# Matrix memory prompt: VectorE weights the scores behind the second update part and norms the rows behind the first

## The reference

```
sc = einsum('bqhd,bshd->bqsh', qc, kc) * wts
num = einsum('bqsh,bshd->bqhd', sc, vc) + a * einsum('bqhk,bhvk->bqhv', qc, C)
den = sum(sc) + a * einsum('bqhk,bhk->bqh', qc, n)
h = num / max(|den|, exp(-m_t))
C_new = decay * C + einsum('blh,blhv,blhk->bhvk', wg, vc, kc)
...
mu = mean(h); var = mean((h - mu)^2)
hn = (h - mu) * rsqrt(var + LN_EPS) * norm_g
hs = (hn + skip * xc) * silu(z)
```

## Time and profile before

| | us |
|---|---|
| median of 3 runs | 3589.51 |
| lowest, highest | 3588.02, 3593.22 |
| profiled execution | 3588.96 |
| its span, first to last instruction | 3587.2 |
| prompt of the matrix memory, first numerator to last result | 2006.3 to 2378.4 |

### The profile page before, as it was taken

One profiled execution on the slowest core, in us unless ns is written; L12 is line 12 of the kernel. 1 busy time (PEld: TensorE's weight loads), 2 busy tenths in 40 slices (PEclk: granted clock), 3 DMA queues, 4 the chain that ended last, 5 costly groups with the idle time before them and its releaser, 6 DMA issues. The chain is left out here.

```text
span 3587.2 us, 53355 instructions
## 1 busy us (share of the span) xinstructions
PE 3330.5 (93%) x20054; PEld 3156.3 (88%) x20054; DVE 1875.0 (52%) x2806; ACT 1170.1 (33%) x1907; POOL 521.3 (15%) x789
## 2 busy tenths in 40 slices
PE   5548989999999998999998999979999999999997
PEld 4448989999999998999976788879999999999997
DVE  7943554544444546322245666654555555555556
ACT  5232434223332223322244322124443222223222
POOL 2241001000000012000012322210001000000012
PEclk7678999999999999999999999989999999999999
DMA  3445531111111122323359422225534433434433
GB/s 85 132 110 143 162 125 42 42 48 36 42 47 42 42 71 89 125 99 111 107 176 327 139 74 82 73 85 136 163 121 129 130 127 119 130 115 131 130 126 132
DMA packets 398386, 389.53 MB, mean 109 GB/s; under 512 B 45652, under 2 KB 336792, under 8 KB 398040
## 3 DMA queue, kind: packets, MB, share of 16 engines
q1 hardware_dynamic: 372666, 324.06, 29.5%
q0 software_dynamic: 18336, 55.14, 4.7%
q10 hardware_dynamic: 7176, 7.35, 0.7%
HBM read 281.45 MB, written 102.63 MB: 107 GB/s over the span
## 5 line engine op out<-in xcount | busy, mean ns | idle before, releaser
L1242 PE MATMUL pair<-x_head,w_head 128*128 128x384 f32 x2544 | 862.8, 339 | 54.9 <-DVE w_rest L841 30.8
L1242 PE MATMUL pair<-x_rest,w_head 128*128 128x384 f32 x2544 | 855.2, 336 | 0.0
L1242 PE MATMUL pair<-x_head,w_rest 128*128 128x384 f32 x2544 | 855.0, 336 | 0.0
L1532 DVE SCALAR_TENSOR_TENSOR cv<-u,par,cv 128x1024 f32<-128x1024 f32 x176 | 225.6, 1282 | 664.9 <-ACT u L1473 664.9
L841 DVE TENSOR_TENSOR w_rest<-w_raw,w_head 128x1024 fp32r<-128x1024 f32 x260 | 317.7, 1222 | 458.8 <-ACT w_head L837 458.8
L1242 PEld LDWEIGHTS pair<-x_head,w_head 128*128 128x128 f32 x2544 | 481.4, 189 | 75.9 <-issue 58.8
L1242 PEld LDWEIGHTS pair<-x_rest,w_head 128*128 128x128 f32 x2544 | 481.4, 189 | 0.0
L1242 PEld LDWEIGHTS pair<-x_head,w_rest 128*128 128x128 f32 x2544 | 481.3, 189 | 0.0
L837 ACT ACTIVATE w_head<-w_raw 128x1024 fp32r<-128x1024 f32 x260 | 275.8, 1061 | 578.2 <-PE pair L1434 279.4
L1468 ACT ACTIVATE cv<-pair,par 128x384 f32<-128x384 f32 x264 | 177.1, 671 | 616.2 <-PE pair L1242 603.0
L1434 PE MATMUL pair<-a_head,w_head 128*128 128x384 f32 x1056 | 361.4, 342 | 3.9 <-DVE f L1565 2.3
(11 more groups left out here) (487 smaller groups left out, 5017.8 us busy)
## 6 DMA issues: line engine op xcount, KB each, us to landing
w_raw<-in_ffn_w_up_dram SPq DMA_DIRECT2D x88, 512.0 KB, 4.0
hs<-in_state_mlstm_C_dram SPq DMA_DIRECT2D x32, 1024.0 KB, 8.6
c_room<-in_state_mlstm_C_dram SPq DMA_DIRECT2D x64, 512.0 KB, 5.7
out_dram<-c_room SPq DMA_DIRECT2D x64, 512.0 KB, 4.6
w_raw<-in_s_w_glu_dram SPq DMA_DIRECT2D x48, 512.0 KB, 4.2
w_raw<-in_mlstm_w_down_dram SPq DMA_DIRECT2D x48, 512.0 KB, 4.3
w_raw<-in_ffn_w_down_dram SPq DMA_DIRECT2D x44, 512.0 KB, 3.7
w_raw<-in_mlstm_w_up_dram SPq DMA_DIRECT2D x32, 512.0 KB, 4.7
```

The lines of the kernel that those rows point to most:

```text
L1242: m = pe.matmul(out[:, 0:TB], lhs[slot][:, P * k:P * k + P], rhs[:, k, TB * c:TB * c + TB], start=(k == 0 and q == 0), stop=(k == KD - 1 a ...
L1532: ins = dve.scalar_tensor_tensor(out=cp, in0=up[:, j:j + SEQ], scalar=tw, in1=cp, op0=ALU.mult, op1=ALU.add)
```

## The change

It moves two instructions in VectorE's body. The norm of the rows, which stood in front of the four updates, now stands behind the first. The weights of the next step, which stood behind the third update, now stand behind the second. The waits go along with their instructions.

```
-                    ge(dve, powed, c, h, 1, 1)
-                    dve.tensor_scalar(flat(cell.h[y]), flat(cell.h[y]), cell.mv[y][:, 0:1], m[:, 2:3],
-                                      ALU.subtract, ALU.mult).then_inc(normed, 1)
                     for t in range(HT):
+                        if t == 1:
+                            ge(dve, powed, c, h, 1, 1)
+                            dve.tensor_scalar(flat(cell.h[y]), flat(cell.h[y]), cell.mv[y][:, 0:1], m[:, 2:3],
+                                              ALU.subtract, ALU.mult).then_inc(normed, 1)
                         ge(dve, stat, c, h, HT, t + 1)
...
-                        if nxt and t == 2:
+                        if nxt and t == 1:
                             weights(*nxt)
```

## The result

| | before | changed |
|---|---|---|
| median of 5 runs, us | 3589.93 | 3572.24 |
| lowest, highest | 3588.02, 3593.22 | 3570.98, 3572.92 |
| span of the profiled execution | 3587.2 | 3570.5 |

The ratio is 0.9946, with a 95% interval from 0.9935 to 0.9956: 16 to 23 us faster. The forecast was 14.3 faster, down to 3571.5 at the range's end. Against the median on which it was made, 3589.51, the ratio stands for 3570.1, just outside the range. The two medians of the table alone give 0.9951, or 3571.8. Five later runs of the same changed kernel on another occasion gave 3574.4 against 3594.33 (9 runs), ratio 0.9952 (0.9938 to 0.9966), or 3572.3. So the gain is clear, and the last microsecond or two of it is not.

What follows compares the result with a forecast made beforehand. TensorE sets the pace, so the change gives back only its waits for VectorE. 2.35 (first chunk) + 3.3 (11 steps) + 7.5 (loop) + 1.1 (last step) = 14.3 us, to 3575.2 against the median; range 3571.5 to 3583.5.

Steps and rivals of the forecast that it cites:

- The stall and its cause: Steps after the first chunk: part 3's load waits for VectorE's first update, behind queries and norm; 0.30 us a step.
- What is late next: Steps after the first chunk: the second update, releasing part 4's load, becomes the next late one; no stall at 2064.93.
- n = 0.46: The norm's start-to-start time behind the first update, taken short because GpSimd's mask is over; 0.60 would stall 0.10.
- The weights: Weights behind the second update: nothing gained in chunk 1, 0.17 us a step in the loop by freeing the numerator's load.
- The low end: Loop, numerator's load: the weights' earlier place gains 0 if the register instructions themselves cost the 0.17.
- The first chunk: Chunk without memory to multiply: three steps gain 0.75 us each as the copy skips the power wait, the first 0.10.
- The last step: No next queries; the update no longer stands behind the norm waiting for the power: gain 1.09 us.
- The sum: Whole stage: 2.35 + 3.3 + 7.5 + 1.1 = 14.3 us faster; gain of 9 to 17 us at chance 0.72.
- The wait did move to part 4: Rival, 27 steps after the first chunk: slowed update or norm shrinks their 0.20 gain to nothing; 3583.4 or 3586; chance 0.14.
- The blocked norm: Rival: GpSimd blocks the norm behind the first update, n 1.16 to 1.30, 3593 to 3597 us; chance 0.04.

Runs made afterwards that it cites:

- e1: Against the changed kernel, the weights put back behind the third update, so only the norm's move remains: ratio 0.9968 to the kernel before, 8 to 15 us faster.
- e4: Against the changed kernel, an idle second batch statistics pass between first update and norm: ratio 1.0009 to the kernel before, 0 to 6 us slower.
- e2: Against the kernel before, only the weights moved, behind the second update: ratio 0.9993 to the kernel before, loop steps 11.726 us on the mean.
- e5: The changed kernel profiled once more with no edit: first step 9.60 us in place of 7.95, loop steps 11.401.
- e8: Against the changed kernel, the norm moved behind the second update and the weights: ratio 0.9943 to the kernel before, loop steps 11.359 us.

## Why the prediction was right and where it was wrong

**The stall and its cause: right.** Part 3's load waited for update 1 with the norm in front of it. The 0.30 a step is measured as 0.31, in the changed kernel and in e1 alone.

**What is late next: right, and close.** Update 2 was named, with 0.04 to 0.06 of slack at n = 0.46. e4 measured 0.05. The choice of 0.46 over 0.60 rested on the mask being out of the way, and the norm took 0.54, 0.46 start to start. In six of the loop's 16 steps the chain ran late and used the slack up; the forecast had one step of chunk 1 stand for all.

**The weights: right.** Nothing outside the loop, 0.17 in it, by e2. The low end, that register instructions cost it themselves, is excluded.

**The first chunk: right in three steps** (0.77 for 0.75). Its first step was put at 0.10, and e1 and e5 have 0.12 to 0.13 at the same clock. The first profile of the changed kernel showed 1.77, of which 1.65 is the clock.

**The last step: the term that was mis-sized.** This is the step of the prediction that failed. "Gain 1.09" counted the update's move and took the rest of the chain to keep its durations. The move came nearly as forecast: numerator to part 3 fell by 1.19, from 9.38 to 8.19. The durations did not stay: part 3 to the transposes fell by 0.87, from 3.05 to 2.18, and the rest by 0.24, from 7.50 to 7.26, because TensorE ran at the high clock where it had been low. (The 2.18 still hold a wait of 0.34 for update 2; e8, without it, has 1.84.) The row of 3.25 for eight records that take 2.00 elsewhere stood in the earlier trace rows, and the forecast put it into the range's end as something that might go. In each of the ten profiles it goes with the idle time that the change shortens. The term is 1.9 to 2.3.

**The sum.** With the terms of e5, whose first step has the low clock as in the kernel before, the stage gives 2.43 + 1.31 + 7.91 + 2.19 + 2.31 = 16.15 us for the 14.3 of the forecast. The last step makes 1.2 of the difference and the loop 0.4. That would be 3573.4, inside the range. The first profile's start, which was luck, adds 1.65 and leads to 3571.7, still inside. The last 1.6 us down to 3570.1 lie in no step of the stage and are not settled: the kernel before ran between 3583.29 and 3602.31 in one series of 31, so a median of five has an error of some microseconds. A range that stopped 3.7 under the point (the prediction calls it the sum plus 3.5, which is 3571.7) was too narrow on this side for that alone.

**The rivals.** The wait did move to part 4, but only in six steps of the loop: by 0.1 in every fourth, by 0.3 in the first and by 0.05 in the ninth. The blocked norm did not come: the norm's longest was 0.60. The Trainium skill (SBUF — State Buffer, Who interferes with whom) says that a VectorE instruction with one SBUF input, outside the modes that use both ports, does not contend with GpSimd. The trace agrees: the update took 0.74 beside the mask. The section's other rule, that the later instruction fully blocks, fits the rows in a way that the forecast had not read from them. The norm that began 0.31 before the mask's recorded end took 0.06 more than alone, the one of the kernel before, which began 0.40 before it, took 0.14 more. Both fit a port that is held until 0.26 before the mask's recorded end, and so do the exponents of the earlier trace rows, whose own 0.29 begin 0.21 before GpSimd's end. That is a reading of three rows, and no run tested it.

## What to carry to other kernels

In a chain of double-buffered parts, order the releasing engine by who waits first: the update that frees a buffer goes ahead of work that is wanted microseconds later, and how far the next release may slide can be read beforehand from start-to-start times, here to 0.01 us in the step that was read, while six of the 27 steps behind chunk 0 ran later than that one and wanted more slack. Idle time of the moving engine elsewhere in the step is no cover for an instruction put into such a chain. Where the change shortens an idle gap of TensorE, ask whether the records behind the gap run at the low clock; if they do, the gap's end is worth more than its length.

## What was not expected of the hardware

TensorE's clock at the stage's start, behind 2.46 to 2.56 us of idle time, fell to the low level in eight of ten profiles and stayed high in two, with the same program on either side (first step 9.60 and 7.95 us). At the stage's end the idle time of 2.33 us was followed by a low granted clock in three of three profiles, and that of 1.13 us or less by 1.00 in seven of seven.

Part 3's weight load ran 0.11 ahead of its matmul where it had nothing to wait for (2059.39 and 2059.50). Where it had to sit a wait out, both start together (2064.40 in the earlier trace rows), and parts 3 and 4 took 1.84 in place of 1.74: 0.10 us of the load were bare.

In the loop, the numerator's load came 0.22 us behind the end of the weights (2161.48 and 2161.70); outside it, with weights that ended as late, 0.06 (2066.52 and 2066.58). The loop's row has register instructions there, which carry the waits. That they are what makes the difference is read from the two places; no run put a wait without them into the loop. The 0.17 us a step are gone when the weights come early (e2).
